# Hybrid SSD/attention block with MoE on one core: the second MoE stage applies its gate row on VectorE as an expert's rows leave PSUM

## What is computed

```python
y = hier_moe(f_l, *moe_args)            # top-1 group, then top-2 of its 8 experts; 32 experts in all
x_lat = x_lat + g2 * y                  # g2: one row of 1024 gate values, the same for all tokens
# inside hier_moe, for a token with experts e0, e1 and weights w0, w1:
# y = w0 * E(e0) + w1 * E(e1),  E(e) = (silu(f @ w_gate[e]) * (f @ w_up[e])) @ w_down[e]
```

## Time and profile before

| | |
|---|---|
| median of 3 runs | 1826.73 us (1826.66 to 1832.74) |
| the profiled execution: its own time | 1825.31 us |
| its span, first to last instruction | 1823.3 us |
| mean granted TensorE clock | 0.967 of 2.4 GHz |
| busy: TensorE / VectorE / ScalarE / GpSimd | 1541.9 / 528.1 / 413.2 / 254.4 us |
| second MoE stage, first gate matmul to last down matmul | 1330.9 to 1800.0 us of the span |

### The profile page before, as it was taken

How to read it: one execution, slowest core, us unless ns; L and a number is a source line. 1 busy time by engine, 2 the same in 40 slices (tenths; PEclk the granted TensorE clock), 3 DMA queues, 4 the chain that set the end, 5 groups by cost and what they waited for, 6 DMA issues and landing times.

```text
span 1823.3 us, 21658 instructions
## 1 busy us (share of the span) xinstructions
PE 1541.9 (85%) x8634; PEld 818.6 (45%) x8634; DVE 528.1 (29%) x1102; ACT 413.2 (23%) x828; POOL 254.4 (14%) x267
## 2 busy tenths in 40 slices
PE   3999999999999899887777777598899887777773
PEld 2433445566544465443344443244455544344341
DVE  2433347777733330000000000647520000000001
ACT  2221146888610111000000001327110100000000
POOL 2000013443310001101001011311011101001001
PEclk9899999999999899999999999799999999999997
DMA  9477767997350699999999997941579999999994
GB/s 360 174 262 297 291 217 205 313 319 260 108 208 13 216 401 419 421 422 423 421 421 421 422 420 295 340 157 48 218 299 392 420 421 421 421 421 420 420 421 172
DMA packets 166140, 579.73 MB, mean 318 GB/s; under 512 B 22290, under 2 KB 77986, under 8 KB 143296
## 3 DMA queue, kind: packets, MB, share of 16 engines
q1 hardware_dynamic: 145072, 531.25, 73.6%
q0 software_dynamic: 15248, 27.62, 4.5%
q10 hardware_dynamic: 5760, 20.06, 3.4%
HBM read 550.60 MB, written 49.77 MB: 329 GB/s over the span
## 4 chain that ended last, share of the span: by engine, by line
PE 49%; DMA 40%; DVE 5%; ACT 3%; issue 2%; SPq 0%; ACTq 0%; POOL 0%; POOLq 0%; DVEq 0%
DMA mem<-in_moe_w_down_dram 36%; PE bank L588 9%; PE bank L1781 8%; PE bank L1768 6%; PE bank L937 6%; PE bank L882 3%; PE bank L2028 3%; PE bank L331 2%; PE bank L905 2%; DMA mem<-in_mod_w_dram 2%; PE bank L2128 2%; ACT mem L987 1%; PE bank L900 1%; PE bank L2075 1%; PE bank L1379 1%
## 5 line engine op out<-in xcount | busy, mean ns | idle before, releaser
L1768 PE MATMUL bank<-mem 128*64 128x256 f32 x4160 | 472.7, 382 | 88.7 <-DMA mem<-in_moe_w_up_dram 39.4
L1768 PEld LDWEIGHTS bank<-mem 128*64 128x64 f32 x4160 | 303.2, 137 | 258.3 <-DMA mem<-in_moe_w_up_dram 60.8
L1781 PE MATMUL bank<-mem 128*64 128x512 f32 x1040 | 252.8, 631 | 89.6 <-DMA mem<-in_moe_w_down_dram 80.9
L1924 DVE COPY mem<-bank 128x256 f32<-128x256 f32 x65 | 27.6, 425 | 688.9 <-PE bank L1775 688.9
L1719 POOL DMA_INDIRECT ys_dram<-mem x65 | 64.8, 996 | 862.6 <-ACT mem L1874 479.3
L1874 ACT ACTIVATE mem<-bank 128x512 f32<-128x512 f32 x65 | 38.8, 597 | 610.5 <-PE bank L1781 610.5
L1781 PEld LDWEIGHTS bank<-mem 128*64 128x64 f32 x1040 | 75.5, 143 | 224.7 <-issue 131.9
L588 PE MATMUL bank<-mem 128*128 128x512 f32 x384 | 172.8, 603 | 1.5 <-DMA mem<-in_ssd_w_in_dram 1.5
L588 PEld LDWEIGHTS bank<-mem 128*128 128x128 f32 x384 | 71.9, 192 | 100.0 <-issue 96.7
L882 PE MATMUL bank<-mem 128*128 128x512 f32 x256 | 115.2, 593 | 0.0
L937 PE MATMUL bank<-mem 128*128 128x512 f32 x256 | 112.3, 595 | 1.8 <-issue 0.9
(11 more groups left out here) (278 smaller groups left out, 1399.0 us busy)
## 6 DMA issues: line engine op xcount, KB each, us to landing
mem<-in_moe_w_up_dram SPq DMA_DIRECT2D x65, 2048.0 KB, 27.2
mem<-in_moe_w_down_dram SPq DMA_DIRECT2D x65, 2048.0 KB, 26.8
mem<-in_moe_w_gate_dram SPq DMA_DIRECT2D x65, 2048.0 KB, 26.4
mem<-in_mod_w_dram SPq DMA_DIRECT2D x24, 2048.0 KB, 8.7
ys_dram<-consts SPq DMA_DIRECT2D x54, 512.0 KB, 7.8
mem<-in_ssd_w_in_dram SPq DMA_DIRECT2D x10, 2048.0 KB, 9.6
mem<-ac_dram ACTq DMA_DIRECT2D x32, 512.0 KB, 5.7
mem<-in_ssd_w_out_dram SPq DMA_DIRECT2D x4, 2048.0 KB, 11.7
```

Of the source, the lines that this page charges most:

```text
L1768: mm = nc.tensor.matmul(bank[half * BR:(half + 1) * BR, 0:HF], lhsT=x[:, k], rhs=w[:, k, half * HF:(half + 1) * HF], start=(k == 0), stop= ...
L1781: mm = nc.tensor.matmul(bank[half * BR:(half + 1) * BR, :], lhsT=ht[:, k % 2, k // 2 * BR:(k // 2 + 1) * BR], rhs=w[:, k, half * COLS:(hal ...
```

## The change

In layer 1 alone, VectorE instead of ScalarE takes an expert's rows out of bank 4, and multiplies them with the gate row on the way (`gated`). The row it needs is half of the gate row on partitions 0 to 63 and the other half on 64 to 127, because the down product lies in the bank in that form: `gate2h`, 128 x 512. It is loaded as two transfers by GpSimd's queue in `norm2_pool(1)`, after the wait for the last of VectorE's shares of the heads (`at_n`); the load of the 128 x 1024 row at L1727 goes in layer 1. VectorE's round j becomes `x_side(j + 1)` and then `gated(j)`, which waits for down j. ScalarE's `h_side` does nothing in layer 1. At the end, ScalarE's step and VectorE's three become two on VectorE: x += w0 * first rows, x += w1 * second rows. One turned tile of the router's input (`fT`) moves to other space, so that the gate row can lie where it was. Layer 0 is as it was.

```diff
--- before.py
+++ after.py
@@ -1131,11 +1131,12 @@
         M0 = A_BCT
         NR = EG + E
         gate2 = region(M0, 2048, "p (s d) -> p s d", s=2)
+        gate2h = region(M0 + 1024, COLS)
         mA = [region(M0 + at, n * D, "p (s d) -> p s d", s=n) for at, n in ((2048, 2), (7168, 1))]
         mB = [region(M0 + at, n * D, "p (s d) -> p s d", s=n) for at, n in ((4096, 2), (10240, 1))]
         gain2 = region(M0 + 6144, D)
         frow = [[region(M0 + at, D) for at in b] for b in ((7168, 8192), (2048, 4096))]
-        fT_at = [[M0 + 9216, M0 + 10240], [M0 + 3072, M0 + 1024]]
+        fT_at = [[M0 + 9216, M0 + 10240], [M0 + 3072, M0 + 8192]]
         wrt = [region(M0 + at, KD * NR, "p (k n) -> p k n", k=KD) for at in (11264, 1712)]
         brt = region(M0 + 11552, NR)
         r_at = [M0 + 11588]
@@ -1254,6 +1255,12 @@
             pool.dma_start(brt[:, EG:], a["moe_b_router"][l:l + 1, :].to_broadcast([P, E])).then_inc(n2_in, 16)
             for s in range(ns):
                 pool.dma_start(mB[l][:, s, :], mod_dram[l, s:s + 1, 3 * D:4 * D].to_broadcast([P, D])).then_inc(n2_in, 16)
+            if l:
+                pool.wait_ge(at_n, 2 * QH)
+                for half in range(2):
+                    c = 5 * D + half * COLS
+                    pool.dma_start(gate2h[half * BR:(half + 1) * BR, :],
+                                   mod_dram[1, 0:1, c:c + COLS].to_broadcast([BR, COLS])).then_inc(n2_g2, 16)
             for t in range(tiles[l]):
                 i = base_t[l] + t + 1
                 pool.wait_ge(n2_ms, i)
@@ -1723,7 +1730,7 @@
             for q in range(3):
                 gather(q)
             mixed(pool, l, nt - 1, 1)
-            for s in range((2, 1)[l]):
+            for s in range((2, 0)[l]):
                 pool.dma_start(gate2[:, s, :], mod_dram[l, s:s + 1, 5 * D:6 * D].to_broadcast([P, D])).then_inc(n2_g2, 16)
             pool.wait_ge(rt_slot, 2 * l + 2)
             pool.wait_ge(ys_zero, N_ZERO)
@@ -1868,6 +1875,8 @@
                 nc.scalar.activation(sil, psum[2 * (b % 2)][:, 0:HF], ACT.Silu).then_inc(moe_sil, 1)
 
             def h_side(j, i=None):
+                if l:
+                    return
                 act.wait_ge(moe_down, at_round(i, BODIES, MB[l] + j + 1))
                 if j >= 2:
                     act.wait_ge(moe_ys[j % 2], at_round(i, 16 * BODIES // 2, 16 * (YB[l][j % 2] + j // 2)))
@@ -1893,8 +1902,9 @@
                     turned(0, 1).then_inc(ov_step[l], 1)
                     act.wait_ge(ov_step[l], i * OVN + 6)
                     nc.scalar.activation(sil, psum[0][:, 0:HF], ACT.Silu).then_inc(ov_step[l], 1)
-                    act.wait_ge(ov_step[l], i * OVN + 11)
-                    nc.scalar.activation(yb[:, 0, :], psum[4][:, :], ACT.Copy).then_inc(ov_step[l], 1)
+                    if l == 0:
+                        act.wait_ge(ov_step[l], i * OVN + 11)
+                        nc.scalar.activation(yb[:, 0, :], psum[4][:, :], ACT.Copy).then_inc(ov_step[l], 1)
                     act.wait_ge(ov_step[l], i * OVN + 12)
                     store(rows_of(P, i + (E // 2 + NB[l] - E)), 0, ov_st[l])
                     act.wait_ge(ov_st[l], (i + 1) * 32)
@@ -1919,13 +1929,28 @@
                     dve.wait_ge(moe_hT, at_round(i, BODIES, MB[l] + b))
                 nc.vector.tensor_tensor(hid, sil, psum[2 * (b % 2) + 1][:, 0:HF], ALU.mult).then_inc(moe_h, 1)
 
+            def gated(j, i=None):
+                if j == 0:
+                    dve.wait_ge(n2_g2, 16 * 4)
+                dve.wait_ge(moe_down, at_round(i, BODIES, MB[l] + j + 1))
+                if j >= 2:
+                    dve.wait_ge(moe_ys[j % 2], at_round(i, 16 * BODIES // 2, 16 * (YB[l][j % 2] + j // 2)))
+                nc.vector.tensor_tensor(yb[:, j % 2, :], psum[4][:, :], gate2h, ALU.mult).then_inc(moe_ya, 1)
+
             def h_side(j, i=None):
                 dve.wait_ge(moe_hT, at_round(i, BODIES, MB[l] + j + 1))
                 nc.vector.tensor_copy(hT[:, j % 2].rearrange("p c m -> p (c m)"), psum[7][:, 0:2 * P]).then_inc(moe_hc, 1)
 
+            def body(j, i):
+                x_side(j + 1, i)
+                if l:
+                    gated(j, i)
+
             x_side(0)
-            rounds(dve, l, lambda j, i: x_side(j + 1, i), lambda j: after_route_dve(dve, l, j))
+            rounds(dve, l, body, lambda j: after_route_dve(dve, l, j))
             h_side(NB[l] - 1)
+            if l:
+                gated(NB[l] - 1)
             n_ov = ov_count(dve, l)
             with dve.If(n_ov > 0):
                 with dve.Fori(0, n_ov) as i:
@@ -1936,10 +1961,13 @@
                     dve.wait_ge(ov_step[l], i * OVN + 9)
                     nc.vector.tensor_copy(hT[:, 0].rearrange("p c m -> p (c m)"), psum[7][:, 0:2 * P]).then_inc(
                         ov_step[l], 1)
+                    if l:
+                        dve.wait_ge(ov_step[l], i * OVN + 11)
+                        nc.vector.tensor_tensor(yb[:, 0, :], psum[4][:, :], gate2h, ALU.mult).then_inc(ov_step[l], 1)
 
         def combine_rows_dve(dve, l, t):
             first, second = (v[:, t] for v in cy)
-            dve.wait_ge(n2_g2, (16 * 2, 16 * 3)[l])
+            dve.wait_ge(n2_g2, 16 * 2)
             dve.wait_ge(cb_s, base_t[l] + t + 1)
             link(dve, nc.vector.scalar_tensor_tensor(first, second, r_w[:, 1, t:t + 1], first, ALU.mult, ALU.add))
             link(dve, nc.vector.tensor_tensor(first, first, gate2[:, t // 2], ALU.mult))
@@ -2374,8 +2402,11 @@
             norm2_dve(dve, 1)
             moe_dve(dve, 1)
             for t in range(NTL):
-                combine_rows_dve(dve, 1, t)
-                combine_add_dve(dve, 1, t)
+                dve.wait_ge(cb_in[t], 32 * 2)
+                link(dve, nc.vector.scalar_tensor_tensor(xin[:, t], cy[0][:, t], r_w[:, 0, t:t + 1], xin[:, t],
+                                                         ALU.mult, ALU.add))
+                nc.vector.scalar_tensor_tensor(xin[:, t], cy[1][:, t], r_w[:, 1, t:t + 1], xin[:, t],
+                                               ALU.mult, ALU.add).then_inc(cb_x, 1)
 
         @block.sync
         def _(sp):
@@ -2443,8 +2474,6 @@
             attn_act(act)
             norm2_act(act, 1)
             moe_act(act, 1)
-            for t in range(NTL):
-                combine_act(act, 1, t)
 
         @block.tensor
         def _(pe):
```

## The result

| | before | changed |
|---|---|---|
| median of 20 runs | 1828.05 us (1824.58 to 1832.74) | 1834.53 us (1829.18 to 1838.25) |
| ratio | | 1.0029, 95% interval 1.002 to 1.0038 |
| the profiled execution: own time, span | 1825.31, 1823.3 us | 1829.24, 1827.4 us |

By the ratio the change costs 5.3 us (0.29% of 1828; interval 3.7 to 6.9), which is within 0.5%. The forecast was no change to that measure, with +3.2 us; the sign is right, and the size is just under the interval. The two medians lie 6.5 us apart and the two means 5.4. The forecast was made from the first three runs of before: 1826.7 x 1.0029 is 1832.0 us, well inside the range (1822.8 to 1834.5), while the changed kernel's own median, 1834.53, stands on the range's upper end.

The account below looks back on a forecast made before the run. Bound by when the weight stream starts, which waits for TensorE's gate 3; 3.7 + 1.3 + 1.7 + 0.1 - 3.6 = +3.2 us on the 1826.7 median gives 1829.9 us, range 1822.8 to 1834.5.

Parts of the forecast that it names:

- What bounds the stage: Second MoE stage: the weight stream's start counts, and a later gate 3 makes all following loads later, one for one.
- Part 1 behind the eviction of block 0: VectorE, round 1: the routing's first part waits for down 0 and its eviction, so gate 2 starts 3.7 us later.
- Part 2 behind the eviction of block 1: VectorE, round 2: overflow-list steps no longer prepared beside down 1, delaying gate 3 by 1.3 us.
- The clock: TensorE ahead of gate 2: 4.6 us of idleness lets the clock fall once, costing 1.7 us; bounds 0 and 3.4.
- The second fall: TensorE in front of gate 3: another clock fall, counted only in the clock term's upper bound of 3.4 us.
- The end: Behind the gathers: two VectorE steps per tile save 3.6 us; the last eviction on VectorE adds 0.1.
- The later rounds and GpSimd's queue: Other evictions hidden by the weight stream, GpSimd's wait and two issues hidden by its idleness: 0 us together.
- The hidden head: Rival, chance 0.20: part 1 does not delay gate 3, only the end's saving is left, 1823.3 us.
- The half clock that stays: Rival, chance 0.05: clock stays down from gate 2 until gate 3 is over, +15.9 us in all, 1842.6 us.
- The rounds do not pay: Rival denied here, chance 0.03: VectorE's eviction delays the turned rows in 15 later pairs, 10.4 us on top, 1840.
- Gate 2's idle stretch: Sign in the profile after: over 4 us of idleness in front of gate 2, released by VectorE.
- Unit 14: Sign: issue of this gate matrix load, which waits for gate 3 to free its slot, at about 1375.5 us.

Follow-up runs that it names:

- part1_first: Changed kernel with part 1 of VectorE's routing work ahead of the eviction of block 0 alone; ratio to before 0.9992.
- evict_thrice: Changed kernel with two more products of bank 4 and the gate row ahead of each eviction from round 3 on; ratio to before 1.0044.
- wait_only: Kernel before, with VectorE also waiting for down j in rounds 0 and 1 of the second MoE stage; ScalarE still evicts; ratio 1.0026.
- parts_first: Changed kernel with VectorE's routing parts 1 and 2 ahead of the evictions of blocks 0 and 1; 1826.63 us, ratio to before 0.9981.
- end_only: Kernel before with only the end changed to VectorE's two steps per tile, gate row left out in layer 1; ratio to before 0.9977.

## Why the prediction was right, and which term was too small

- **What bounds the stage.** Right. The stream lasted 431.2 to 431.7 us in nine of ten profiles, for heads from 37.9 to 46.4 us, so what the head gained or lost was neither taken back nor added to behind it.
- **Part 1 behind the eviction of block 0:** forecast +3.7, measured +3.85; part 1 itself took 4.30 us in place of 4.18, and the rest is handovers.
- **Part 2 behind the eviction of block 1:** forecast +1.3, measured +1.34.
- **The clock:** forecast +1.7 for one fall, measured +3.1 for two (1.38 + 1.68). This is the term that was too small. The second fall, ahead of gate 3, was only a bound. In the three profiles that have that stretch at its full 3 us without filling, the group behind it was slowed each time (8.81 in the changed kernel, 8.42 in part1_first, 8.81 in evict_thrice), while after 2.25 us in wait_only it was not. After the stretch ahead of gate 2 (4 to 4.8 us) the clock fell each of the four times it was there without filling: groups of 8.47 to 8.81 us. The Trainium skill, "TensorE: Matmul & The Clock Gate", section "HAM oscillation", tells of a kernel that waits before each group of its matmuls and pays for a fall of the clock every time. The changed kernel's trace agrees: each of its two stretches had a fall of its own, and I priced one.
- **The end:** forecast -3.6, measured -3.5 in the changed kernel and -3.6 alone. The difference is the size of the last eviction's +0.1, but the ends of the kernels with the same end scatter from 19.64 to 20.39 us, so it is not shown.
- **The later rounds and GpSimd's queue:** forecast 0, measured +0.4 in the stream, which is within what the other profiles scatter; in evict_thrice the rounds took 38.6 us more of VectorE's time for 1.0 us.
- **Sum:** forecast +3.2; by the stretches +5.1 without the start of the stage, which is 1.0 us earlier in this one profile; it lies anywhere in 9 us, so nothing can be read from that. The ratio says +5.3.
- **The rivals.** The hidden head needed 5 us of slack at unit 14; there was none, and parts_first and wait_only rule it out from both sides. The half clock that stays did not come: each fall was over within its group, and down 1 between them took its 3.65 us. The rounds do not pay, as evict_thrice shows, up to the last one. That the time counts as no change would have come out under the hidden head too, 3.5 us below before; it is the stretches, not that verdict, that bear out the mechanism.
- **Signs that came otherwise.** Gate 2's idle stretch was to be released by VectorE; the bracket says "issue", and only the starts around it show VectorE. Unit 14 was forecast 44.6 us after gate 0 and came after 46.2, by the second fall.

## What to carry to other kernels

When work moves to another engine, look at what stands behind it in that engine's program, and not only at its duration. A wait for a late event, put ahead of work that used to run beside that wait, delays this work by the time it had run ahead, less the slack it had: here 0.69 us of work made gate 2 late by 3.85 us, and 3.04 of them came with the wait alone (part 1 had run 3.6 us ahead of down 0's end and had 0.6 of slack). Here the same instructions in another order turned +0.3% into -0.2%. In a stage that is bound by a stream, find where the stream starts, and read from the idle queue whether the start waits for an engine; up to there every microsecond counted here, and behind it 38.6 us of VectorE's time cost 1.0. And where TensorE's idle stretches are filled, the filling has to end before the stretch does: 5 and 1 matmuls gained 3.1 us, 8 and 3 gained nothing.

## What was not expected of the hardware

The time from the start to gate 0 varied from 1329.4 to 1338.2 us in ten profiles, while the stream behind it stayed within 0.6 us in nine of them. A comparison of two spans would have had end_only (1826.6 us) slower than before (1823.3), where the many runs show it 0.23% faster. The scatter has no single place: the time to layer 0's first gate matmul varies by 3.2 us, layer 0's MoE stage by 2.5, and the part from there to gate 0 by 4.8 (196.7 to 201.5). What makes them vary stays open.
